# Sixty-four moving columns instead of 128 in the doubling inverse of a delta rule kernel

## The reference, cut to what matters

```python
a_mat = beta[..., :, None] * jnp.einsum("bhnid,bhnjd->bhnij", k, k) * dec_strict
eye = jnp.eye(DN_CHUNK, dtype=jnp.float32)
rhs = jnp.concatenate([beta[..., None] * v, (beta * jnp.exp(g))[..., None] * k], -1)
sol = lax.linalg.triangular_solve(eye + a_mat, rhs, left_side=True, lower=True, unit_diagonal=True)
```

## Time and profile before

| what | value |
|---|---|
| median of three runs | 2072.08 us |
| the profiled execution, first to last instruction (the page gives this span and no other time of it) | 2075.5 us |
| PE (matmuls) busy | 1941.3 us, 94% |
| PEld (weight loads) busy | 1762.3 us, 85% |
| DVE / ACT / POOL busy | 50% / 38% / 15% |
| head loop of the DeltaNet | from about 1410 to 1700 us |

### The profile page before, as it was taken

How to read it: one execution, slowest core, us unless ns; L and a number is a source line. 1 busy time by engine, 2 the same in 40 slices (tenths; PEclk the granted TensorE clock), 3 DMA queues, 4 the chain that set the end, 5 groups by cost and what they waited for, 6 DMA issues and landing times.

```text
span 2075.5 us, 33299 instructions
## 1 busy us (share of the span) xinstructions
PE 1941.3 (94%) x11932; PEld 1762.3 (85%) x11932; DVE 1037.7 (50%) x1819; ACT 797.8 (38%) x1279; POOL 304.5 (15%) x378
## 2 busy tenths in 40 slices
PE   4999999876889999999999999998999989999998
PEld 2988988775678989988999889977888878899997
DVE  2533333899773334355444357734435445644444
ACT  0322322546443333235443235454333333444422
POOL 0100000567330000012000015002112114200000
PEclk7999999998899999999999999999999998999999
DMA  8677665122137665652445653420000012244441
GB/s 277 205 225 228 193 202 155 51 82 61 30 123 221 214 217 172 189 150 83 121 126 172 189 144 83 131 70 9 5 8 8 5 48 72 71 128 132 126 128 43
DMA packets 369952, 253.99 MB, mean 122 GB/s; under 512 B 9715, under 2 KB 350307, under 8 KB 369891
## 3 DMA queue, kind: packets, MB, share of 16 engines
q1 hardware_dynamic: 369891, 253.21, 40.7%
HBM read 250.55 MB, written 2.62 MB: 122 GB/s over the span
## 4 chain that ended last, share of the span: by engine, by line
PE 74%; DVE 15%; issue 7%; ACT 1%; DMA 1%; POOL 1%; SPq 0%; DVEq 0%; ACTq 0%; POOLq 0%
PE bank L1211 22%; PE bank L1213 20%; PE bank L1212 20%; PE bank L1259 4%; DVE conv L901 3%; DVE tap_odd L901 2%; DVE h_full L852 2%; DVE w_lo L817 1%; DMA mod_raw<-in_w_mod 1%; DVE rstd L870 1%; DVE r L860 1%; PE bank L1408 1%; DVE r L1189 1%; POOL h_lo L484 1%; DVE h_full L866 1%
## 5 line engine op out<-in xcount | busy, mean ns | idle before, releaser
L1211 PE MATMUL bank<-h_hi,w_hi 128*128 128x384 f32 x1920 | 657.7, 343 | 37.6 <-POOL h_lo L484 21.5
L1213 PE MATMUL bank<-h_hi,w_lo 128*128 128x384 f32 x1920 | 645.4, 336 | 0.0
L1212 PE MATMUL bank<-h_lo,w_hi 128*128 128x384 f32 x1920 | 645.2, 336 | 0.0
L817 DVE TENSOR_TENSOR w_lo<-w_raw,w_hi 128x1024 fp32r<-128x1024 f32 x336 | 429.9, 1302 | 260.4 <-ACT w_hi L601 257.4
L601 ACT ACTIVATE w_hi<-w_raw 128x1024 fp32r<-128x1024 f32 x336 | 344.2, 1050 | 318.2 <-PE bank L1213 221.5
L1211 PEld LDWEIGHTS bank<-h_hi,w_hi 128*128 128x128 f32 x1920 | 362.7, 189 | 76.0 <-issue 32.4
L1212 PEld LDWEIGHTS bank<-h_lo,w_hi 128*128 128x128 f32 x1920 | 363.0, 189 | 0.0
L1213 PEld LDWEIGHTS bank<-h_hi,w_lo 128*128 128x128 f32 x1920 | 362.7, 189 | 0.0
L1211 PE MATMUL bank<-act_hi,w_hi 128*128 128x384 f32 x704 | 241.9, 344 | 0.0
L1213 PE MATMUL bank<-act_hi,w_lo 128*128 128x384 f32 x704 | 236.6, 336 | 0.0
L1212 PE MATMUL bank<-act_lo,w_hi 128*128 128x384 f32 x704 | 236.4, 336 | 0.0
(11 more groups left out here) (257 smaller groups left out, 2021.6 us busy)
## 6 DMA issues: line engine op xcount, KB each, us to landing
w_raw<-in_ffn_w_in SPq DMA_DIRECT2D x176, 512.0 KB, 4.7
mod_raw<-in_w_mod SPq DMA_DIRECT2D x144, 512.0 KB, 4.9
w_raw<-in_ffn_w_out SPq DMA_DIRECT2D x64, 448.0 KB, 4.7
w_raw<-in_ffn_w_out SPq DMA_DIRECT2D x32, 512.0 KB, 4.6
w_raw<-in_dn_w_in SPq DMA_DIRECT2D x32, 512.0 KB, 4.0
w_raw<-in_cv_w SPq DMA_DIRECT2D x24, 512.0 KB, 3.8
w_raw<-in_dn_w_out SPq DMA_DIRECT2D x8, 512.0 KB, 4.0
out<-x_rows SPq DMA_DIRECT2D x6, 256.0 KB, 2.1
```

Of the source, the lines that this page charges most:

```text
L817: dve.tensor_tensor(w_lo[:, slot], w_raw[:, slot], w_hi[:, slot].bitcast(F32), ALU.subtract).then_inc(w_lo_ready, 1)
L1211: pe.matmul(ps, w_hi[:, w_slot, k], a_hi, start=start, stop=False)
L1212: pe.matmul(ps, w_hi[:, w_slot, k], a_lo, start=False, stop=False)
L1213: return pe.matmul(ps, w_lo[:, w_slot, k], a_hi, start=False, stop=stop)
```

## The change

Both products of a level get a column pattern on their moving operand and on their output. The number of instructions, the weights, the waits and all other engines' code stay as they are.

```diff
                                 else:
-                                    mm = pe.matmul(bank[d][:, t * P:(t + 1) * P], decay[:, d, t], inv[:, d, t], start=True, stop=True)
+                                    mm = pe.matmul(every_other(bank[d][:, t * P:(t + 1) * P], n, d), decay[:, d, t],
+                                                   every_other(inv[:, d, t], n, d), start=True, stop=True)
                             mm.then_inc(p_ready, 1)
...
                                 for t in range(NT):
-                                    mm = pe.matmul(bank[4 + d][:, t * P:(t + 1) * P], step_p[:, d, t], inv_t[:, d, t], start=True, stop=True)
+                                    mm = pe.matmul(every_other(bank[4 + d][:, t * P:(t + 1) * P], n, 1 - d), step_p[:, d, t],
+                                                   every_other(inv_t[:, d, t], n, 1 - d), start=True, stop=True)
                                 mm.then_inc(t_ready, 1)
```

## The result

The changed kernel takes 2140.35 us (median of four runs, 2139.61 to 2158.31) against 2071.48 us before (four runs, 2069.73 to 2072.26): a ratio of 1.0352, with a 95% interval from 1.0326 to 1.0378. It is slower by some 69 us, where I had forecast 3.3 us less. Everything that follows is about one number of the page, the granted clock, and about how long it stays low once it has fallen. (The page gives it as PEclk, in tenths of full speed.)

What follows compares the result with a forecast made beforehand. The prediction took direction 0's chain, with TensorE nearly full beside it, as the bound. Gains of 0.29, 0.053 and 0.073 us made 0.42 a head, 3.3 for eight: 2072.08 to 2068.8 us, range 2065.6 to 2072.6.

Steps and rivals of the forecast that it cites:

- What bounds the kernel: Head loop: direction 0's chain without a gap, 3.72 us a level, with TensorE nearly full beside it, 14.42 of 14.91 us.
- the distance of the records: Products P and T: loads start every 0.112 us, set by the weight load alone, so fewer moving columns don't shorten it.
- The sum: Gain over the levels of the inverse: 0.42 us a head, 3.3 us for eight heads.
- The part of T: Second product of each level: its last result, and the join, transposes and copy after it, come 0.053 us earlier.
- that of P: First product: 0.02 us a level, from bounds of 0.01 and 0.053; nothing at level 1.
- The single level: One level of the inverse, from P to the next P: 3.72 us becomes 3.65.
- One sign I had named: PE records of P and T get about 0.053 us shorter, 275 to some 222 ns.
- The pattern's price: Columns in runs of 2 at level 1, of 4 at level 2: no price taken; slower writes as a rival, 5%.
- The clock: Rival at heads' beginnings: one to three more heads fall to half clock, 1.4 us each, 2070.2 to 2073.0 us; 14%.
- the clock falling inside the levels: Rival on the slower side: the clock falls inside the levels, or in six or more heads; together 3%.
- The deduction from the median: The 3.3 us, worked out in a profiled execution of 2075.5 us, was carried to the runs' median of 2072.08: 2068.8 us.

Runs made afterwards that it cites:

- the last two runs: Kernel before with filling products and half the output rows left out: half the weights with all columns, 2078.80 us; half of both weights and moved columns, 2041.01 us.
- the filled change: Changed kernel plus constant products that compute nothing, seven in TensorE's wait in each head and nine ahead of the first: 2069.80 us, ratio 0.9989 to before.
- the filled kernels: Six kernels with added constant products: the change 2069.80 us, before 2071.69, level 1 full 2071.55, T alone narrow 2069.66, half weights 2078.80, half of both 2041.01.

## Why the prediction was wrong, point by point

**What bounds the kernel, and the distance of the records: right.** One chain of 3.72 us a level with the engine nearly full beside it; loads and moved columns both at 0.11 us. The loads of the changed kernel keep it, and the last two runs show both limits.

**The sum: right in kind, a good quarter too large.** I had 0.42 us a head and it is 35.89 - 35.56 = 0.33. The part of T, 6 x 0.053 = 0.32, measured 0.25; that of P, 5 x 0.02 = 0.10, measured 0.04 by itself and 0.08 beside T. The single level was exact, 3.65 us. One sign I had named was wrong: the mean length of the records at full clock is still 273 to 275 ns. Their ends come 0.05 us earlier after the loads all the same, as ScalarE's and VectorE's starts show. T's first record starts 0.05 us after its first load (1480.03 to 1479.98) where it was 0.09 before (1467.91 to 1467.82), so with few columns it seems to be the recorded start that moves and not the length.

**The pattern's price: right.** None that can be measured. The rule of the Trainium skill that I set against the change (PSUM — Partial Sum Buffer, Specifications: a non-contiguous pattern slows matmuls significantly) isn't borne out by these runs: all 128 columns in runs of 2 and more gave a ratio of 1.0000.

**The clock: this step failed.** The rival was named, its place was right (the beginning of a head) and so was its number (one to three more heads; four heads have a fall now, where two had one before). Its price was wrong by a factor of twelve. I took 1.4 us for a fall from a kernel in which the level right behind it has 128 columns and the clock is back at 1530.5, and applied it to a kernel in which exactly these products are changed. A fall's price has two parts, the slower work per us and the time until the clock is back; the change left the first alone (1.4 us lost in 3.4 us at half clock before, 17.3 in 41 after, 0.41 and 0.42 us per us) and stretched the second from 3.5 to some 41 us, and to 51 in head 0. I gave "the clock falling inside the levels" 3% with others and no price, though 17 us a head would have been easy to work out: six levels at nearly twice their 3.65 us; 6 x (6.44 - 3.65) = 16.7 in the runs.

The Trainium skill (TensorE: Matmul & The Clock Gate, What's actually happening) says that the engine starts throttled and that activity releases it. I had drawn on this section for the fall and not for the return. In this trace a high busy share in the profile went along with the low clock (34.16 of 34.20 us busy at 1.2 GHz), and in the filled change's it stood right ahead of a fall (3.40 of 3.40 us busy), so the busy share doesn't show what the clock will do.

**The deduction from the median.** The forecast was carried from a profiled execution to the runs' median as if both had the same falls of the clock. They had not: the profiled one was some 6 us longer than the median, and most of that it lost ahead of the head loop, where head 0 started at 1410.11 us and in the other kernels between 1403.7 and 1406.9. This didn't matter for the result, but it spoilt the expectations of the filled kernels.

## What to carry to other kernels

Halving the moved columns of a matmul whose 128 columns of fp32 weights take as long to load wins only the tail of the last one in a group, here 0.05 us; to shorten the stream, both sides must shrink. Before making TensorE's work lighter, look for the places at which the granted clock falls and ask which work brings it back: if it is the work that is changed, a fall of 3 us can become one of 40. A few products that compute nothing, put where the engine waits anyway, or the first two levels left at full width, held the loss down for next to no cost (2069.80 and 2073.17 us); level 3 alone at full width still left 18 us (2089.14). None of them was clearly faster than the kernel before.

## What the runs showed that I had not expected

- The same stream of narrow products runs at full clock when it starts there and at half clock when it starts there: 35.56 and 52.9 us for neighbouring heads of one execution.
- At half clock the fp32 weight loads of 128 columns are 0.21 us apart, even though only 64 columns are moved: the loads slow down with the clock.
- In the filled kernels the clock still fell in some heads, right behind 3.4 us in which TensorE was busy without a gap, most of them in products with weights of 16 or 32 rows.
- Taking 64 columns in P costs more through the clock than taking them in T, 6.8 us at half clock for each fall against 3.4.
- With half of the weights and all columns a head is 0.3 us longer than before, 36.2 against 35.9 us. No run was made on why.
